# Row homes in use until eight rows are left, layer 2's first loads and splits moved behind the row stage

## The reference

```python
s_top, i_top = lax.top_k(s, PEER_TOPK)                 # 8 heads, 16 of each
expert = jnp.take_along_axis(cand_idx, pos, axis=-1)   # 128 experts per token
g = jax.nn.softmax(best, axis=-1)
act = jax.nn.gelu(jnp.einsum('td,thkd->thk', xb, u[expert]), approximate=False)
out = jnp.einsum('thk,thkd->td', (g * act), v[expert])
h = h + out                       # end of layer 1, then rms_norm
...
h = _rmsnorm(x, norm_pre)         # layer 2
cols = h @ w_in                   # its first pieces: dnq, dnk, dnv
```

## Time and profile before

| | us |
|---|---|
| median of 3 runs (1271.07 to 1272.14) | 1271.2 |
| the profiled execution | 1271.57 |
| its span, first to last instruction | 1269.8 |

### The profile page before, as it was taken

How to read it: one execution, slowest core, us unless ns; L and a number is a source line. 1 busy time by engine, 2 the same in 40 slices (tenths; PEclk the granted TensorE clock), 3 DMA queues, 4 the chain that set the end, 5 groups by cost and what they waited for, 6 DMA issues and landing times.

```text
span 1269.8 us, 13273 instructions
## 1 busy us (share of the span) xinstructions
PE 1099.2 (87%) x4932; PEld 741.3 (58%) x4932; DVE 782.1 (62%) x1573; ACT 469.1 (37%) x983; POOL 293.7 (23%) x313
## 2 busy tenths in 40 slices
PE   9999999978894976868758776769999999999997
PEld 9888877644342432323323332323888989888886
DVE  6597546627547658577494764445585655755574
ACT  5657322222222223222232221123467434574333
POOL 1054103233244332533325334131001000000001
PEclk9999999999898897988979879998999999999999
DMA  6543259899899999999999999997244332444522
GB/s 207 197 167 133 83 155 382 331 384 422 324 379 420 422 422 420 421 421 421 422 421 422 420 422 421 413 413 321 91 163 149 130 134 102 165 167 155 228 84 113
DMA packets 61841, 363.98 MB, mean 287 GB/s; under 512 B 6848, under 2 KB 17360, under 8 KB 20304
## 3 DMA queue, kind: packets, MB, share of 16 engines
q0 software_dynamic: 36864, 268.45, 51.3%
q1 hardware_dynamic: 24448, 94.48, 21.0%
q10 hardware_dynamic: 464, 0.20, 0.1%
HBM read 361.01 MB, written 2.10 MB: 286 GB/s over the span
## 4 chain that ended last, share of the span: by engine, by line
PE 59%; DMA 18%; DVE 13%; ACT 3%; POOL 3%; issue 2%; DVEq 0%; POOLq 0%; ACTq 0%
PE ps L1969 18%; PE ps L2132 18%; DMA big<-in_uv,big 13%; PE ps L1935 9%; PE ps L1902 3%; DMA ring<-in_uv,big 2%; DMA actT<-in_uv,big 2%; DVE big L1546 2%; DMA ring<-in_peer_w_q 2%; PE ps L2020 2%; DVE lo L1300 2%; POOL big L799 1%; PE ps L2083 1%; ACT big L1013 1%; PE ps L1865 1%
## 5 line engine op out<-in xcount | busy, mean ns | idle before, releaser
L2132 PE MATMUL ps<-big 128*128 128x512 f32 x556 | 270.6, 633 | 91.7 <-ACT big L1013 91.7
L1546 DVE CUSTOM_DVE_ANT_0 big<-big,ps 128x1024 f32<-128x1024 f32 x139 | 167.9, 1219 | 146.0 <-DMA big<-in_uv,big 146.0
L2132 PEld LDWEIGHTS ps<-big 128*128 128x128 f32 x556 | 111.2, 204 | 242.6 <-issue 133.5
L1969 PE MATMUL ps<-hi,x 128*128 128x512 f32 x704 | 225.2, 394 | 1.6 <-DVE lo L1300 1.4
L799 POOL DMA_INDIRECT big<-in_uv,big x139 | 131.9, 949 | 274.6 <-PE ps L2132 194.6
L2132 PE MATMUL ps<-ring,big 128*128 128x512 f32 x332 | 158.8, 626 | 31.7 <-ACT big L1013 26.1
L1300 DVE TENSOR_TENSOR lo<-raw,hi 128x2048 fp32r<-128x2048 f32 x60 | 140.4, 2342 | 72.2 <-ACT hi L877 71.8
L1005 ACT ACTIVATE big<-big 128x4 f32<-128x4 f32 (+1 forms) x66 | 13.6, 205 | 428.3 <-DVE big L1546 428.3
L1546 DVE CUSTOM_DVE_ANT_0 ring<-ring,ps 128x1024 f32<-128x1024 f32 x83 | 100.2, 1219 | 85.7 <-DMA ring<-in_uv,big 85.7
L1969 PEld LDWEIGHTS ps<-hi,x 128*128 128x128 f32 x704 | 132.2, 188 | 30.3 <-issue 2.2
L877 ACT ACTIVATE hi<-raw 128x2048 fp32r<-128x2048 f32 x60 | 114.6, 1910 | 69.8 <-PE ps L1969 42.9
(11 more groups left out here) (371 smaller groups left out, 1361.7 us busy)
## 6 DMA issues: line engine op xcount, KB each, us to landing
raw<-in_pieces SPq DMA_DIRECT2D x61, 1024.0 KB, 4.9
ring<-in_peer_w_q SPq DMA_DIRECT2D x8, 1024.0 KB, 7.9
big<-in_up SPq DMA_DIRECT2D x4, 2048.0 KB, 8.6
big<-in_uv,big POOLq DMA_INDIRECT x139
ring<-in_w_mem_kv SPq DMA_DIRECT2D x2, 1024.0 KB, 12.4
ring<-in_uv,big POOLq DMA_INDIRECT x83, 19.4
resid<-in_x SPq DMA_DIRECT2D x2, 512.0 KB, 4.9
raw<-in_pieces SPq DMA_DIRECT2D x2, 512.0 KB, 9.3
```

What stands on the lines that cost most here:

```text
L1546: ins = dve.tensor_tensor_reduce(out=row, in0=row, in1=hn_ps[n], scale=1.0, scalar=0.0, op0=ALU.mult, op1=ALU.add, accum_out=dots[:, n, s: ...
L1969: ins = pe.matmul(o, a, b[:, c], start=(s == 0 and c == 0 and k == 0), stop=(s == 1 and c == HALF - 1 and k == 2))
L2132: ins = pe.matmul(ps[:, 4 + 2 * n + half, :], diag[:, s % DIAGS], row_home[home_of[k]][:, D + half * TILE:D + (half + 1) * TILE], start=(s ...
```

## The change

`LAST_ROWS` goes from 32 to 8, so that the five kept-free homes take rows until eight are left, and the plan of homes changes from row 227 on. With it every `home_free` value of these homes rises, on which SP's loads of `dnq0` and `dnq1` wait. ACT's two `hi` halves of `dnq0` move from behind batch 61 to behind the last batch; DVE's two `lo` halves move from six rows ahead of the last dot to behind the last dot, ahead of `add_peer(1)`. Nothing else changes; the arithmetic is the same.

```diff
--- before.py
+++ after.py
@@ -44,7 +44,6 @@
 BATCH_ENDS = [*range(BATCH, ROWS - BATCH + 1, BATCH), ROWS - 2, ROWS - 1, ROWS]
 BATCHES = len(BATCH_ENDS)
 BATCHES_0 = SLOTS // BATCH
-SPLIT_BATCH = SLOTS // BATCH * NT - 2
 DIAGS = 2 * BATCH
 
 
@@ -395,7 +394,7 @@
         FIRST_ROW = {"early0": 0, "early1": 0, "early2": 0, "early3": 0, "ring3": 4, "ring4": 5, "ring5": 6, "query1": 7, "mixT": 8,
                      "ring2": 13, "actT": 22, "query0": 23, "keys": 24, "memT": 56, "ring0": 56, "ring1": 57, "mkv": 62}
         WEIGHTS_IN_MIXT = range(9, 48)
-        LAST_ROWS = 32
+        LAST_ROWS = 8
         KEPT_FREE = ("ring0", "ring1", "ring2", "ring4", "mixT")
         home_of, rows_in = [], {name: [] for name in row_home}
         for k in range(ROWS):
@@ -1049,12 +1048,11 @@
                     exponentials(u + 2)
                 if b == BATCHES_0 + 4:
                     squares(0)
-                if b == SPLIT_BATCH - 1:
-                    act.wait_ge(v_done, home_free("ring2"))
-                    act.wait_ge(tile_loaded[0], piece_loads("dnq0"))
-                    act.activation(hi2[:, 0, 0:D], raw2[:, 0, 0:D], ACT.Copy).then_inc(hq0a_then_dnq0a_hi, 1)
-                    act.activation(hi2[:, 0, D:2 * D], raw2[:, 0, D:2 * D], ACT.Copy).then_inc(piece_hi, 1)
-
+
+            act.wait_ge(v_done, home_free("ring2"))
+            act.wait_ge(tile_loaded[0], piece_loads("dnq0"))
+            act.activation(hi2[:, 0, 0:D], raw2[:, 0, 0:D], ACT.Copy).then_inc(hq0a_then_dnq0a_hi, 1)
+            act.activation(hi2[:, 0, D:2 * D], raw2[:, 0, D:2 * D], ACT.Copy).then_inc(piece_hi, 1)
             squares(1)
             piece_split_hi("dnq1")
             act.wait_ge(rows_loaded, 48)
@@ -1572,13 +1570,12 @@
                     dot_rows(PICKS * u, PICKS * u + PICKS)
                 else:
                     scale_rows(0)
-                    dot_rows(PICKS * u, ROWS - 6)
+                    dot_rows(PICKS * u, ROWS)
                     dve.wait_ge(v_done, home_free("ring4"))
                     dve.wait_ge(hq0a_then_dnq0a_hi, 2)
                     dve.tensor_tensor(lo2[:, 0, 0:D], raw2[:, 0, 0:D], hi2[:, 0, 0:D].bitcast(F32), ALU.subtract)
                     dve.wait_ge(piece_hi, piece_no["dnq0"] + 1)
                     dve.tensor_tensor(lo2[:, 0, D:2 * D], raw2[:, 0, D:2 * D], hi2[:, 0, D:2 * D].bitcast(F32), ALU.subtract).then_inc(piece_lo, 1)
-                    dot_rows(ROWS - 6, ROWS)
                 if u + 2 < UNITS:
                     search_unit(u + 2)
```

## The result

The changed kernel takes 1264.02 us (median of 6 runs, 1262.74 to 1265.52) against 1271.67 for the kernel before (6 runs): ratio 0.9941, 95% interval 0.9928 to 0.9955, or 7.65 us less between the medians (5.7 to 9.2 by the interval). A later set of runs on one more chip gave 0.9960 (0.9946 to 0.9974). The forecast was 1264.2 in a range of 1260.6 to 1268.3. The profiled execution took 1265.52, its span is 1263.8, 6.0 less than before.

A forecast was written before the change was run, and what follows sets the result against it. Row gathers were taken to set the pace before layer 2, sharing DMA with loads. Pace -10.65, collision +5.1, PE backlog -2.9 and hi/lo +1.5 gave -7.0 us: median 1264.2, range 1260.6 to 1268.3.

The forecast's parts named there:

- What bounds: Before layer 2, row gathers set the pace at 2.484 us a row, and layer 2's loads share their DMA engines.
- The loads leave the old place: Rows 216 to 229 no longer share the DMA engines with layer 2's first loads: 8.2 us regained.
- The loads at the new place: SP issues the loads at 866.4, delaying the last gathers; row 255 comes 5.1 us late, its dot at 880.5.
- 2.5 us for `dnk0` and -2.9 for PE's backlog: Rows 253 to 255 regain 2.5 us; last dot to add_peer shrinks 2.9 us as PE is no longer behind.
- PE not behind at row 255: PE catches up in the weighted sum's tail; its matmuls end at 884.5, 4.0 us after the last dot.
- rival (2): PE at half clock in a batch after 61: add_peer at 886.4 to 887.8, time 1265.3; chance 0.13.
- Rival (1): PE at half clock in batch 61: loads out at 869.6, row 254 on time, gain 9.6 us, 1261.6; chance 0.15.
- `hi` and `lo`, 1.5 us: The halves of dnq0 behind the last dot lie uncovered, so add_peer starts at 886.0 instead of 884.5.
- The depth of homes at nothing: Rows up to 250 reuse homes 17 rows old instead of 12; the extra depth costed at nothing.
- The small loads hidden, with 3 us to spare: rows, ba_w and wsT land by 882, 887 and 888, before ACT needs them at 891.5.
- Rival (4): The small load becomes the bound, delaying ACT's copy_hi_T by 15.4 us: 8.4 us slower, 1279.6; chance 0.04.
- Rival (3): The loads take all their 8.2 us before row 255: dot at 883.6, gain 3.9 us, 1267.3; chance 0.08.

The follow-up runs named there:

- experiment 2: The kernel before with LAST_ROWS = 8 and nothing else, the hi and lo halves left early: 1280.27 us, ratio 1.0078.
- experiment 1: The changed kernel with LAST_ROWS back at 32, so loads go out early and only the halves stay late: 1270.29 us, ratio 0.9992.
- experiment 8: The changed kernel with LAST_ROWS = 32, but SP still waiting for row 244's batch before issuing dnq0 and dnq1: 1265.28 us, ratio 0.9942.
- experiment 11: The changed kernel itself run and profiled again on another chip, nothing altered: 1264.86 us, ratio 0.9960 to the kernel before.
- experiment 4: The changed kernel with DVE's two lo halves of dnq0 moved behind add_peer(1) and normed(1): 1263.08 us, ratio 0.9934.
- experiment 3: The changed kernel with SP holding dnq0 and what follows until row 255 has landed: 1263.34 us, ratio 0.9941.
- experiment 9: The changed kernel with lo halves behind add_peer and batches of two from row 224, loads not held: 1267.14 us, ratio 0.9970.
- experiments 5 and 12: Changed kernel with loads held until row 255 landed and lo halves behind add_peer: 1263.44 us; the same plus batches of two from row 224: 1261.87 us.
- experiment 7: The changed kernel with loads held until row 255 landed, lo halves behind add_peer, batches of two from row 224: 1260.31 us, ratio 0.9898.
- experiment 10: The changed kernel with loads held, lo halves behind add_peer, nine unused PE multiplications behind each of batches 44 to 61: 1263.83 us, ratio 0.9940.

## Why the prediction was right

*What bounds.* The pace of the gathers, 2.48 us a row, and that the loads share it: right, and unchanged in every trace, save where DVE stood for a load (experiment 2).

*The loads leave the old place* (forecast: 8.2 us regained between rows 216 and 229). Mis-sized: 7.2. One step of 3.45 us remains in the changed kernel, where no load is near; the kernel before had it too (a step between dots 1 us longer than its neighbours, at the same row), and I had booked it on the loads. This term is the whole miss of `add_peer`'s time: forecast 886.0, measured 886.98.

*The loads at the new place* (SP at 866.4, rows +0.3, +2.8, +5.1). Right but for that 1.0: SP at 867.39, rows +0.3, +2.8, +5.0. Reading the new collision off the rows of the old one, at the same distance from a batch's end, was good to 0.1 us. The title puts these loads behind the row stage; they are behind the issue of the last gathers and ahead of the landing of four.

*2.5 us for `dnk0` and -2.9 for PE's backlog.* Here the sum was right and its parts were not causes. The kernel before was bound by PE from row 251 on, so that `dnk0`'s collision, which touches only later rows, cost nothing (experiment 1: last dot 2.5 earlier, time unchanged). The sum takes 2.5 us off the last dot for it; but the 6.9 us that it measures from that dot to `add_peer` are themselves shorter by the same 2.5 than they would be without the collision, so nothing is won by it. What was won is row 251's dot, 7.2 earlier (873.64 to 866.45), less 1.15 on the way from it to `add_peer`, where the new place and the halves cost more than PE's queue did.

*PE not behind at row 255* (matmuls end at 884.5, 4.0 after the last dot). Half wrong: rival (2) came true, batch 62 began at half clock and PE ended at 885.7, 4.3 after the last dot. It cost nothing, since the `lo` halves ended later still. Rival (2) had been priced at 0.4 to 1.8 us; in this execution it was 0. Experiment 8, with batch 62 at full clock, shows PE idle before row 255 as forecast. Rival (1) came in the second trace of the changed kernel (experiment 11), and was mis-sized: batch 61 was 1.4 us longer and not 3.2, row 254 did not escape, the halves did not hide under PE, and `add_peer` gained 1.3 us, not 2.6.

*`hi` and `lo`, 1.5 us.* The last dot to `add_peer`, 5.5 forecast, 5.55 measured. Of it 1.3 us lay behind the matmuls, 1.2 by experiment 4.

*The depth of homes at nothing.* Right to 0.2 us (experiment 8).

*The small loads hidden, with 3 us to spare.* Right in the result, and the spare time was larger: `ba_w` landed at 880.5 instead of 887, and `wsT`, the last of the three, at 883.2 instead of 888 (14.0 after its issue). With no gather beside it (experiment 3) `ba_w` landed 7.7 us after its issue, together with the megabytes in front of it. Rival (4), this load as the new bound, is refuted, and so is its premise that the slowness of 36 us was its own: it was the gathers'. The prediction also says that the trace disagrees with the rule of turns of the Trainium skill ("DMA: Bandwidth & Descriptors", "Queues, rings and completion order"). It does not: a turn of small runs stands behind a turn of gather runs. By that page's 9 to 17 in each, 64 small runs need 4 to 8 turns, and each waits for 9 to 17 gather runs of 0.31 us: 11 to 42 us, an estimate by the rule's figures, with the measured 23.3 inside. Few turns need not be short ones.

*Rival (3), all 8.2 us ahead of the last row,* did not occur; what it would have cost is seen in experiment 9, where the loads go out about seven rows ahead: 6.1 us on the last dot. The 8.2 of the rival contained the 1.0 of row 222.

*The time.* That the median (1264.02) met the forecast to 0.2 us is luck. In the traces the gain was 6.0 us where the sum had 7.0; the medians give 7.65, and on another chip 6.4 (experiment 11), with single executions of one kernel 3 to 6 us apart.

*Same and slower.* Experiment 2 is what the change would have been with only its first half, 9.5 us slower. The prediction names no such case, since the diff moved both.

## What to carry to other kernels

A transfer is out of the way of others only when they have *landed*; here, issued behind the last gathers, it still held up those that were queued. Look for the row that is the last one in the tail of each engine: here PE worked off its queue from row 251 on, so five microseconds saved on rows 253 to 255 were worth one to two, until smaller last batches shortened that queue (experiment 9: 6.1 on the last dot, 5.3 in the medians). When two terms of a sum describe the same wait from its two ends, the sum can be right while neither is a cause; an experiment that removes one of them shows it.

## What was not expected of the hardware

In every trace the step between the dots of rows 221 and 222 is 1.0 us longer than its neighbours (3.42 to 3.47 us instead of 2.48 where no load is near), with the DMA share at 1.00 around it, and all rows behind it stay 1.0 us late. It goes with the row and not with the time, in kernels with 12 and with 17 homes alike. The cause stays open. In the traces of before, after and experiments 5 and 12 a packet of an instruction queue falls 1 to 3 us ahead of the late dot (in the changed kernel between 792 and 793), but another one between 821 and 822 has no late row behind it. Whether it is the addresses that this row fetches or the count of gathers issued by then was not tried either.

`ba_w`, 32 KB in runs of 32 B, landed 36.0 us after its issue beside a full queue of gathers, 11.8 with four gathers still to land, and 7.7 with none (experiment 3).

PE's granted clock fell to half in some gaps of 2.8 us and not in others, in traces of one and the same kernel; with gaps of 1.3 us (experiment 7) or 0.8 us (experiment 10) it stayed at full there. With batches of two and one gap of 5.9 us (experiment 9) it fell again: the eight records behind it took 5.13 us instead of 3.70.
